# Expert bias parts: formed on VectorE from biases loaded ahead of the expert pieces, instead of by ScalarE and GpSimd in turns

## The chip, the cores and the metric

One core of a Trainium2 chip runs the whole kernel. Its engines each follow their own list of instructions and meet at semaphores: TensorE (PE in the profile) multiplies, VectorE (DVE) and ScalarE (ACT) work element by element, GpSimd (POOL) builds small tables and starts some transfers, and SyncE (SP) does nothing but wait and start transfers. The metric is the device time of one execution in microseconds (us), taken as the median of several executions.

## The reference

One layer of a transformer is run for two groups of tokens that share their weights: 256 prompt tokens and 64 sample tokens with 512 cached keys. Everything is float32.

```python
x = x + mixed @ w_o                       # mixed: two kinds of attention heads, concatenated
h = rmsnorm(x, g_ffn)                     # 320 tokens of width 1024
logits = h @ w_r + b_r                    # 32 experts, the best 4 of each token are used
for e in range(32):
    g = min(h @ w_gate[e] + b_gate[e], 7)
    u = clip(h @ w_up[e] + b_up[e], -7, 7)
    y = ((u + 1) * (g * sigmoid(1.702 * g))) @ w_down[e] + b_down[e]
    x += combine[:, e] * y
x = x + (p @ w_ple_proj) * sigmoid(rmsnorm(x, g_ple) @ w_ple_gate)
return rmsnorm(x, g_final), and the new keys, values and log-forget rows
```

Each of the three expert matrices has 4 MB per expert, so 32 experts hold some 400 MB that have to be read once from HBM.

## The kernel before

The program has three stages: projections and attention (0 to about 216 us of the profile), output projection and routing (216 to 304 us), and the experts (304 to 1299 us) with a short tail.

**Experts.** An item is up to 64 tokens of one expert. Its weights come as six pieces of 2 MB (two of the gate matrix, two of up, two of down) into a ring of six slots; `early` holds two more. SP starts the load of a piece as soon as PE has used the piece that lay in the slot (`wait_used`, semaphore `piece_used`). Of the first item, pieces 0, 1, 2 and 5 can be loaded once attention has left their slots; pieces 3 and 4 lie where `w_o` is kept, so that they, and behind them in SP's list the two early pieces of the second item, wait for the whole output projection (`wo_ps` 6).

**Biases.** The rows of `b_gate`, `b_up` and `b_down` are added by a matmul. Its stationary operand `sel` picks the expert, its moving operand `bparts` holds all biases as three bfloat16 parts that add up to the float32 value: partitions 0 to 31, 32 to 63 and 64 to 95 each hold one part of the 32 experts' 3072 biases. So SP loads three copies of the biases into `bias32` (nine transfers of 128 KB, lines 409 to 411). A first copy rounds all 96 rows to bfloat16 (`bias_part` 1). Then the rounded values are subtracted in place on the first 64 rows and these are rounded again, and the same once more on the first 32 rows. Before the change ScalarE rounds (lines 685 to 690) and GpSimd subtracts (lines 528 to 531); each waits for the other (`bias_part`, `bias_rest`). `bias32` and `bparts` lie in `area`, where attention keeps its queries and keys, so they can only be filled when PE has read those for the last time.

**What stands around them.** Every engine works through its list in the order in which it is written. On GpSimd the two subtractions stand ahead of the small tables of the routing (lines 533 to 546), the last of which raises `consts` to 3. On VectorE the last work of attention is `new_key_rows` (lines 1191 to 1197), which copies the transposed new keys out; then comes a wait for `consts` 3 (line 1314), three small copies into `ident_e`, and `add_out` (line 1287), which adds a block of the output projection to `X`. On PE the order is: three blocks of the output projection (`project_out`), the transposes of `normed_to_T(0)` (line 952), which need both `add_out` of the first 128 tokens, the fourth block, `logits`, and so on to the routing, the first `gather` of tokens and the first item. On ScalarE `squares` for the norm follow behind the bias copies.

**SP** in this stretch: the two loads of `w_o`, a wait for all ten transfers of new keys and values to the outputs (`out_dma`), piece 0, a wait for the end of attention, pieces 1, 2, 5, the nine biases, a wait for `wo_ps` 6, pieces 3, 4 and the two early ones.

Of the kernel before, what the change touches and what calls it, by code (L numbers as in the profile page):

```python
# [31 lines left out]
ALU = mybir.AluOpType  # L32
ACT = mybir.ActivationFunctionType
# [3 lines left out]
D = 1024  # L37
# [15 lines left out]
NE, TOPK = 32, 4  # L53
# [40 lines left out]
def build(nc, A, O):  # L94
    ctx = ExitStack()
    with ctx:
# [3 lines left out]
        def sem(name):  # L100
            return ctx.enter_context(nc.semaphore(name))
# [37 lines left out]
        def cut(n):  # L139
            nonlocal a  # L140
            a += n
            return area[:, a - n:a]
# [4 lines left out]
        bias32 = area[0:3 * NE, 0:3 * D]  # L147
        bparts = cut(3 * D // 2)[0:3 * NE, :].bitcast(BF16).rearrange("p (r n) -> p r n", r=3)
# [81 lines left out]


        x_in, g_in, small_in, kc_in, vc_in, ff_in, tab_in = [sem(n) for n in ("x_in", "g_in", "small_in", "kc_in", "vc_in", "ff_in", "tab_in")]
        bias_in, bias_part, bias_rest, rel_out, rel_rows, rel_in, out_dma = [sem(n) for n in ("bias_in", "bias_part", "bias_rest", "rel_out", "rel_rows", "rel_in", "out_dma")]
        wqk = [sem(f"wqk{i}") for i in range(CHUNK_SLOTS)]
        wv_in, wout_in = sem("wv_in"), sem("wout_in")
        consts = sem("consts")
# [9 lines left out]
        kr_ps, kr_sb = sem("kr_ps"), sem("kr_sb")  # L246
# [95 lines left out]
        def down(tile, n):  # L342

            return tile[n * SLOTS:(n + 1) * SLOTS, :]

        @block.sync
        def _(sp):
# [23 lines left out]
            def load(e, s, into=None, done=None):  # L371

                src = wexp[s // 2][bass.ds(e, 1), s % 2].rearrange("a p c n -> (a p) c n") if not isinstance(e, int) else wexp[s // 2][e, s % 2]
                sp.dma_start((ring if into is None else into)[:, s, :].rearrange("p (c n) -> p c n", c=QC), src).then_inc((done or wst)[s], 16)  # L374
# [25 lines left out]
                sp.dma_start(wout[h], w_o[:, :, h * GW:(h + 1) * GW]).then_inc(wout_in, 16)  # L400


            sp.wait_ge(out_dma, OUT_PRE)
            load(0, 0)
            sp.wait_ge(mixed_ok, 1)
            sp.wait_ge(o_ps, NO)
            for s in (1, 2, 5):
                load(0, s)
            for r, nm in enumerate(("b_gate", "b_up", "b_down")):
                for k in range(3):  # L410
                    sp.dma_start(bias32[k * NE:(k + 1) * NE, r * D:(r + 1) * D], A[nm][0]).then_inc(bias_in, 16)  # L411
            sp.wait_ge(wo_ps, 2 * NT)
            for s in (3, 4):
                load(0, s)
# [42 lines left out]
        def _(pool):  # L457
            g = nc.gpsimd
            n = 0
# [56 lines left out]
            for t in range(NT):  # L516
                r = ROWS[t]
# [6 lines left out]
            for x, nm in ((0, "fk"), (1, "dk")):  # L524
                g.dma_start(O[nm + "_p"][0, 0].rearrange("(t p) h -> p t h", p=P), krow[x][:, 0:2, :]).then_inc(out_dma, 16)
                g.dma_start(O[nm + "_s"][0, 0], krow[x][0:DEC, 2, :]).then_inc(out_dma, 16)

            for k in (2, 1):
                pool.wait_ge(bias_part, 3 - k)
                v = bias32[0:k * NE, :]  # L530
                g.tensor_tensor(v, v, bparts[0:k * NE, :, :].rearrange("p r n -> p (r n)"), ALU.subtract).then_inc(bias_rest, 1)  # L531

            pool.wait_ge(o_sb, NO)
            g.iota(iota_s, [[1, SLOTS]], base=1, channel_multiplier=0, allow_small_or_imprecise_dtypes=True)
# [9 lines left out]
            for h in range(2):  # L544
                ins = g.memset(down(far[:, :], h), float(2 * FAR + h))
# [17 lines left out]
            for t in range(NT):  # L563
                r = ROWS[t]
# [8 lines left out]
        def _(act_e):  # L573
            s = nc.scalar
            n = 0
# [106 lines left out]
            for j, c in enumerate((4, 5, 6, 7, 0, 1, 2, 3)):  # L682
                act_e.wait_ge(hT_ps, DC + j + 1)
                s.activation(hT[:, c, :], ps[:, c, 0:NTOK], ACT.Copy).then_inc(hT_sb, 1)
            parts = bparts.rearrange("p r n -> p (r n)")
            act_e.wait_ge(bias_in, 16 * 9)
            s.activation(parts, bias32, ACT.Copy).then_inc(bias_part, 1)
            for k in (2, 1):
                act_e.wait_ge(bias_rest, 3 - k)
                s.activation(parts[0:k * NE, :], bias32[0:k * NE, :], ACT.Copy).then_inc(bias_part, 1)  # L690
            for t in range(NT):
                act_e.wait_ge(x1_ok, 2 * (t + 1))
                squares(1, t)
# [1 line left out]
            for t in range(NT):  # L695
                r = ROWS[t]
# [29 lines left out]
            for t in range(NT):  # L726
                r = ROWS[t]
# [17 lines left out]
            for t in range(NT):  # L745
                r = ROWS[t]
# [11 lines left out]
        def _(pe):  # L758
# [31 lines left out]
            for t in range(NT):  # L790
                r = ROWS[t]
# [227 lines left out]
            def tokens(i):  # L1019

                pe.wait_ge(rows_sb, lin(i, 1, 1))
                columns_of(tok_rows, TOK_BANK).then_inc(tokT_ps, 1)
# [18 lines left out]
            def trip(i):  # L1041

                pe.wait_ge(tok_ok, lin(i, 1, 1))
                pe.wait_ge(sel_ok, lin(i, 1, 1))
                bias(0, G_BANK)
                product(i, 0, tokT, G_BANK)
                if i is FIRST:
                    tables()
                product(i, 1, tokT, G_BANK)
                bias(1, U_BANK)  # L1050
                product(i, 2, tokT, U_BANK)
                product(i, 3, tokT, U_BANK)
                if i is not FIRST:
                    pe.wait_ge(y_sb, lin(i, 1))
                bias(2, Y_BANK)
                gather(item(i, 1))
                pe.wait_ge(act_ok, lin(i, 1, 1))
                columns_of(act, ACT_BANK).then_inc(actT_ps, 1)
                tokens(item(i, 1))
                pe.wait_ge(actT_ok, lin(i, 1, 1))  # L1060
                product(i, 4, actT, Y_BANK)
                product(i, 5, actT, Y_BANK)
# [11 lines left out]
            mm(ps[:, TAB_BANK, 100:101], below[:, :], need, True, True)  # L1074
            mm(ps[0:1, TAB_BANK, 101:102], need, ones[:, 0:1], True, True).then_inc(rank_ps, 1)
            tokens(FIRST)
            pe.wait_ge(bias_part, 3)
            trip(FIRST)
            pe.wait_ge(items_ok, 1)
            n1 = pe.value_load(cnti[0:1, 0:1], min_val=NE - 1, max_val=ITEMS - 1)  # L1080
# [5 lines left out]
            for c in range(2):  # L1086
                for t in range(NT):
                    r = ROWS[t]
# [27 lines left out]
            for t in range(NT):  # L1116
                r = ROWS[t]
# [19 lines left out]
        def _(dve):  # L1137
            V = nc.vector
            n = 0

            def link(ins):

                nonlocal n
                n += 1
                ins.then_inc(dve_seq, 1)
                dve.wait_ge(dve_seq, n)
# [20 lines left out]
            for t in range(NT):  # L1167
                r = ROWS[t]
                ins = V.tensor_tensor(zz[0:r, t, :], ps[0:r, 6, t * FH:(t + 1) * FH], bf[0:r, :], ALU.add)
# [5 lines left out]
            for i in range(2):  # L1175
                ins = V.tensor_tensor(dlam[:, 128 * i:128 * i + 64], dlam[:, 128 * i:128 * i + 64], dlam[:, 128 * i + 64:128 * i + 128], ALU.mult)
# [14 lines left out]
            def new_key_rows():  # L1191
                for g8 in range(8):
                    x, m = g8 // 4, g8 % 4
                    dve.wait_ge(kr_ps, g8 + 1)
                    V.tensor_copy(krow[x][:, 0:2, m * P:(m + 1) * P],
                                  ps[:, g8 % 4, 0:2 * P].rearrange("p (t n) -> p t n", t=2)).then_inc(kr_sb, 1)
                    V.tensor_copy(krow[x][0:DEC, 2, m * P:(m + 1) * P], ps[0:DEC, g8 % 4, 2 * P:3 * P]).then_inc(kr_sb, 1)
# [58 lines left out]
            for p in range(PAIRS):  # L1256
# [4 lines left out]
                if p == 5:  # L1261

                    dve.wait_ge(o_sb, DH)
                    for t in range(NT):
                        r = ROWS[t]
                        if t == 2:
                            dve.wait_ge(sub_ss, 1)
                        for hh in range(DH):
                            v = H[0:r, t, GW + hh * P:GW + (hh + 1) * P]
                            ins = V.scalar_tensor_tensor(squares_of[0:r, t % 2, hh * P:(hh + 1) * P], v, 1.0, v, ALU.mult, ALU.mult,  # L1270
                                                         accum_out=ssd[0:r, t, hh:hh + 1])
                        ins.then_inc(sub_ss, 1)
                if p == 6:
                    dve.wait_ge(sub_rstd, NT)
                    for t in range(NT):
                        r = ROWS[t]
                        for hh in range(DH):
                            v = H[0:r, t, GW + hh * P:GW + (hh + 1) * P]
                            ins = V.scalar_tensor_tensor(v, v, ssd[0:r, t, hh:hh + 1], subg[0:r, :], ALU.mult, ALU.mult)
                    ins.then_inc(mixed_ok, 1)  # L1280
            new_key_rows()

            def add_out(t, h):
                r = ROWS[t]
                dve.wait_ge(wo_ps, 2 * t + h + 1)
                src = ps[0:r, 2 * t + h, :] if t < 2 else down(ps[:, 4, :], h)
                V.tensor_tensor(X[0:r, t, h * GW:(h + 1) * GW], src, X[0:r, t, h * GW:(h + 1) * GW], ALU.add).then_inc(x1_ok, 1)
# [27 lines left out]
            for k in range(3):  # L1315
                rr = slice(k * NE, (k + 1) * NE)
                ins = V.tensor_copy(ident_e[rr, :], ident[rr, rr])
# [16 lines left out]
            for t in range(NT):  # L1334
                r = ROWS[t]
                ins = V.tensor_reduce(place[0:r, t, :], masks[0:r, :, t, :].rearrange("p k e -> p e k"), AXX, ALU.add)
            link(ins)
            for t in range(NT):
                r = ROWS[t]
                ins = V.tensor_scalar(slotv[0:r, t, 0:NE], place[0:r, t, :], -1.0, tok4[0:r, t:t + 1], ALU.mult, ALU.add)  # L1340
# [4 lines left out]
            for t in range(NT):  # L1345
                r = ROWS[t]
                ins = V.scalar_tensor_tensor(posm[0:r, t, 0:NE], ps[0:r, POS_BANKS[t], t * NE:(t + 1) * NE], 1.0, mask[0:r, t, :], ALU.add, ALU.mult)
# [64 lines left out]
            for t in range(NT):  # L1412
                r = ROWS[t]
                dve.wait_ge(w_exp, t + 1)
                link(V.reciprocal(wsum[0:r, 2, t:t + 1], wsum[0:r, 1, t:t + 1]))
                ins = V.tensor_scalar(w4[0:r, t, :], w4[0:r, t, :], wsum[0:r, 2, t:t + 1], None, ALU.mult)
# [35 lines left out]
            for t in range(NT):  # L1452
                r = ROWS[t]
                dve.wait_ge(pj_sb, t + 1)
                for h in range(2):
# [3 lines left out]
                    ins = V.tensor_tensor(X[0:r, t, c], tsig[0:r, c], X[0:r, t, c], ALU.add)  # L1459
# [44 lines left out]
```

## Time and profile before

| | us |
|---|---|
| median of three executions | 1383.2 (1380.15 to 1385.09) |
| profiled execution | 1379.01 |
| its span, first to last instruction | 1377.2 |
| PE busy in the span | 1207.5 (88%) |
| DVE, ACT, POOL busy | 296.5, 189.0, 87.9 |
| read from HBM | 469.32 MB, 351 GB/s over the span |

The profile page gives shares over the whole span; the stages differ. In its row of 40 slices (34.4 us each) the transfers run at 427 to 430 GB/s from the 13th slice to the 36th, and at 5 GB/s in the eighth. A wait in brackets in the timeline is idle time of that engine before the instruction, with what ended it.

### The profile page before, as it was taken

The numbers are of one execution on the slowest core, as the hardware profiler recorded it, in microseconds if no ns is written. First come the engines' busy times: TensorE is split into PE (matmuls) and PEld (weight loads), VectorE is DVE, ScalarE is ACT, GpSimd is POOL, SyncE is SP. The second block draws the span as 40 slices with busy tenths as digits, with TensorE's granted clock in tenths as the row PEclk, the third lists the DMA queues.
The fourth block names the chain that finished last, engine by engine and source line by source line (L and its number), as shares of the span: only waits on it lengthen the run. The fifth ranks groups of instructions, "written<-read, shape, count | busy, mean of one in ns | idle before, by whom it ended". The sixth has DMA issues, their size and how long they took to land.

```text
span 1377.2 us, 15632 instructions
## 1 busy us (share of the span) xinstructions
PE 1207.5 (88%) x5919; PEld 496.2 (36%) x5919; DVE 296.5 (22%) x844; ACT 189.0 (14%) x419; POOL 87.9 (6%) x148
## 2 busy tenths in 40 slices
PE   5999979489999899988898988889998889998866
PEld 4565664243333333332233332233333223333322
DVE  2343450142211111111111111111111111111153
ACT  2232441210100010000001000001000000100122
POOL 6000100400000000000000000000000000000000
PEclk9999987789999999999999999999999999999978
DMA  9460158059999999999999999999999999999941
GB/s 294 172 168 16 51 186 312 5 245 371 396 429 427 428 430 429 428 429 429 428 429 429 429 428 428 428 428 429 429 428 427 430 429 429 428 427 428 369 150 39
DMA packets 64555, 478.88 MB, mean 348 GB/s; under 512 B 9136, under 2 KB 26136, under 8 KB 38100
## 3 DMA queue, kind: packets, MB, share of 16 engines
q1 hardware_dynamic: 57968, 462.19, 81.1%
q0 software_dynamic: 4496, 16.02, 3.2%
q10 hardware_dynamic: 2068, 0.37, 0.2%
q8 instruction: 14, 0.23, 0.1%
q14 instruction: 9, 0.07, 0.0%
HBM read 469.32 MB, written 14.47 MB: 351 GB/s over the span
## 4 chain that ended last, share of the span: by engine, by line
DMA 58%; PE 35%; DVE 2%; POOL 1%; ACT 1%; issue 1%; SPq 1%; ACTq 0%; POOLq 0%; DVEq 0%
DMA ring<-in_w_up 54%; PE ps L762 33%; DMA area<-in_b_down 2%; POOL area L531 1%; DMA ring<-expert_rows 1%; PE ps L774 1%; DMA X<-in_x_sample 0%; DMA expert_rows<-area,rowi 0%; DVE X L1437 0%; DMA out_dk_s<-ring 0%; PE ps L1016 0%; PE ps L871 0%; PE ps L873 0%; SPq L374 0%; SPq L411 0%
## 5 line engine op out<-in xcount | busy, mean ns | idle before, releaser
L762 PE MATMUL ps<-ring,area 128*64 128x512 f32 x3232 | 728.0, 597 | 93.3 <-DMA ring<-in_w_up 76.8
L762 PEld LDWEIGHTS ps<-ring,area 128*64 128x64 f32 x3232 | 221.8, 137 | 556.2 <-issue 383.8
L1381 DVE TENSOR_SCALAR area<-ps 128x512 f32<-128x512 f32 x34 | 23.5, 691 | 429.4 <-PE ps L762 429.4
L762 PE MATMUL ps<-ring,hT 128*128 128x512 f32 (+2 forms) x320 | 110.9, 570 | 2.8 <-issue 2.3
L762 PE MATMUL ps<-H,area 128*64 128x512 f32 (+1 forms) x420 | 103.1, 609 | 2.5 <-DVE area L1355 2.5
L558 POOL DMA_INDIRECT expert_rows<-area,rowi x34 | 33.2, 977 | 979.7 <-ACT area L715 979.7
L762 PE MATMUL ps<-area 128*64 128x1 f32 (+6 forms) x756 | 79.0, 285 | 1.7 <-issue 1.2
L1385 DVE TENSOR_SCALAR area<-ps 128x512 f32<-128x512 f32 x34 | 23.5, 692 | 259.5 <-PE ps L762 259.5
L762 PE MATMUL ps<-hT,ring 128*128 128x320 f32 x256 | 74.9, 448 | 0.0
L704 ACT ACTIVATE area<-ps 128x512 f32<-128x512 f32 x35 | 20.9, 597 | 393.4 <-PE ps L762 393.4
L762 PEld LDWEIGHTS ps<-ring,hT 128*128 128x128 f32 (+1 forms) x320 | 46.9, 176 | 61.7 <-issue 58.8
L762 PEld LDWEIGHTS ps<-area 128*64 128x64 f32 (+4 forms) x756 | 38.3, 134 | 66.3 <-issue 64.4
L709 ACT ACTIVATE area<-area 128x512 f32<-128x512 f32 x34 | 21.4, 629 | 264.8 <-DVE area L1381 264.8
L762 PEld LDWEIGHTS ps<-hT,ring 128*128 128x128 f32 x256 | 48.8, 195 | 24.1 <-issue 6.2
L715 ACT ACTIVATE area<-ps 128x512 f32<-128x512 f32 x34 | 20.3, 597 | 244.4 <-PE ps L762 244.4
L762 PEld LDWEIGHTS ps<-H,area 128*64 128x64 f32 (+1 forms) x420 | 27.2, 137 | 65.7 <-issue 63.1
L1016 PE MATMUL ps<-ident,area 128*128 128x128 f32 x276 | 42.5, 297 | 0.0
L1016 PEld LDWEIGHTS ps<-ident,area 128*128 128x128 f32 x276 | 35.9, 210 | 0.5
L1383 DVE TENSOR_TENSOR area<-area 128x512 f32<-128x512 f32 x34 | 23.6, 693 | 23.6 <-ACT area L709 23.6
L1355 DVE TENSOR_SCALAR area<-area 128x64 f32<-128x64 f32 (+1 forms) x108 | 27.0, 308 | 0.9
L660 ACT ACTIVATE ring<-ring,mx 128x128 f32<-128x128 f32 (+2 forms) x48 | 26.3, 552 | 6.7 <-DVE mx L1231 6.6
L762 PE MATMUL ps<-ring 128*128 128x64 f32 (+3 forms) x96 | 17.1, 309 | 10.2 <-ACT ring L643 10.2
(193 smaller groups left out, 556.0 us busy)
## 6 DMA issues: line engine op xcount, KB each, us to landing
ring<-in_w_up SPq DMA_DIRECT2D x68, 2048.0 KB, 25.8
ring<-in_w_down SPq DMA_DIRECT2D x68, 2048.0 KB, 22.6
ring<-in_w_gate SPq DMA_DIRECT2D x66, 2048.0 KB, 25.2
ring<-in_w_in SPq DMA_DIRECT2D x16, 512.0 KB, 8.4
ring<-in_w_in SPq DMA_DIRECT2D x2, 2048.0 KB, 9.6
ring<-in_w_o SPq DMA_DIRECT2D x2, 2048.0 KB, 15.1
early<-in_w_gate SPq DMA_DIRECT2D x2, 2048.0 KB, 19.0
ring<-in_w_ple_gate SPq DMA_DIRECT2D x1, 4096.0 KB, 31.6
```

Source lines behind the costliest of these rows:

```text
L531: g.tensor_tensor(v, v, bparts[0:k * NE, :, :].rearrange("p r n -> p (r n)"), ALU.subtract).then_inc(bias_rest, 1)
L558: g.indirect_dma_start(out=yscr[:, :], out_offset=bass.IndirectOffsetOnAxis(ap=rowi[:, 0:1], axis=0), in_=yrow, in_offset=None, bounds_che ...
L660: last = s.activation(v, v, ACT.Exp, bias=mx[0:r, u, t:t + 1], accum_out=rs[0:r, u, t:t + 1])
L704: s.activation(tok_rows, ps[:, ROWS_BANK, :], ACT.Copy).then_inc(rows_sb, 1)
L709: s.activation(sig, gate, ACT.Sigmoid, scale=ALPHA).then_inc(sig_ok, 1)
L715: s.activation(yrow, ps[:, Y_BANK, :], ACT.Copy).then_inc(y_sb, 1)
L762: return T.matmul(out, lhsT, rhs, start=first, stop=last)
L1016: last = T.transpose(ps[:, b, c * P:(c + 1) * P], rows[:, c::QC], ident[:, :])
L1355: ins = V.tensor_scalar(pick[0:r, t, :], iota_s[0:r, :], posm[0:r, t, bass.ds(e, 1)], first[0:r, bass.ds(lin(i, 1), 1)], ALU.subtract, ALU ...
L1381: V.tensor_scalar(gate, ps[:, G_BANK, :], LIMIT, None, ALU.min).then_inc(g_sb, 1)
L1383: V.tensor_tensor(gate, gate, sig, ALU.mult)
L1385: V.tensor_scalar(up, ps[:, U_BANK, :], LIMIT, -LIMIT, ALU.min, ALU.max).then_inc(up_sb, 1)
```

## The change

SP starts the nine bias loads behind the loads of `w_o`, as soon as PE has made the last transposes of the new keys (`kr_ps` 8), and in front of the wait for `out_dma` and all expert pieces. VectorE makes the three roundings and the two subtractions, in a row behind `new_key_rows` and in front of the wait for `consts` 3. ScalarE and GpSimd have none of it, the semaphore `bias_rest` goes, and PE waits for one signal of `bias_part` in place of three. Data, sizes and all other work stay.

```diff
+            sp.wait_ge(kr_ps, 8)
+            for r, nm in enumerate(("b_gate", "b_up", "b_down")):
+                for k in range(3):
+                    sp.dma_start(bias32[k * NE:(k + 1) * NE, r * D:(r + 1) * D], A[nm][0]).then_inc(bias_in, 16)
             sp.wait_ge(out_dma, OUT_PRE)
             load(0, 0)
             sp.wait_ge(mixed_ok, 1)
             sp.wait_ge(o_ps, NO)
             for s in (1, 2, 5):
                 load(0, s)
-            for r, nm in enumerate(("b_gate", "b_up", "b_down")):
-                for k in range(3):
-                    sp.dma_start(bias32[k * NE:(k + 1) * NE, r * D:(r + 1) * D], A[nm][0]).then_inc(bias_in, 16)
             sp.wait_ge(wo_ps, 2 * NT)
...
-            for k in (2, 1):
-                pool.wait_ge(bias_part, 3 - k)
-                v = bias32[0:k * NE, :]
-                g.tensor_tensor(v, v, bparts[0:k * NE, :, :].rearrange("p r n -> p (r n)"), ALU.subtract).then_inc(bias_rest, 1)
-
             pool.wait_ge(o_sb, NO)
...
-            parts = bparts.rearrange("p r n -> p (r n)")
-            act_e.wait_ge(bias_in, 16 * 9)
-            s.activation(parts, bias32, ACT.Copy).then_inc(bias_part, 1)
-            for k in (2, 1):
-                act_e.wait_ge(bias_rest, 3 - k)
-                s.activation(parts[0:k * NE, :], bias32[0:k * NE, :], ACT.Copy).then_inc(bias_part, 1)
             for t in range(NT):
                 act_e.wait_ge(x1_ok, 2 * (t + 1))
                 squares(1, t)
...
-            pe.wait_ge(bias_part, 3)
+            pe.wait_ge(bias_part, 1)
             trip(FIRST)
...
             new_key_rows()
 
+            parts = bparts.rearrange("p r n -> p (r n)")
+            dve.wait_ge(bias_in, 16 * 9)
+            link(V.tensor_copy(parts, bias32))
+            for k in (2, 1):
+                v = bias32[0:k * NE, :]
+                link(V.tensor_tensor(v, v, parts[0:k * NE, :], ALU.subtract))
+                ins = V.tensor_copy(parts[0:k * NE, :], v)
+                if k == 2:
+                    link(ins)
+            ins.then_inc(bias_part, 1)
```

SyncE's list from the loads of `w_o` to the biases, before; `in_w_gate`, `in_w_up` and `in_w_down` into `ring` are expert pieces, `in_b_...` the biases:

```order
L400 DMA ring<-in_w_o 128x8x512 x2
L374 DMA ring<-in_w_gate 128x4096 x2
L374 DMA ring<-in_w_up 128x4096
L374 DMA ring<-in_w_down 128x4096
L411 DMA area<-in_b_gate 32x1024 x3
L411 DMA area<-in_b_up 32x1024 x3
L411 DMA area<-in_b_down 32x1024 x3
```

The same place of SyncE's list after the change:

```order
L400 DMA ring<-in_w_o 128x8x512 x2
L406 DMA area<-in_b_gate 32x1024 x3
L406 DMA area<-in_b_up 32x1024 x3
L406 DMA area<-in_b_down 32x1024 x3
L374 DMA ring<-in_w_gate 128x4096 x2
L374 DMA ring<-in_w_up 128x4096
L374 DMA ring<-in_w_down 128x4096
```

The nine biases have moved past four pieces, which are 8 MB; nothing else has moved.

VectorE's list from the last copies of `new_key_rows` to `add_out`, before:

```order
L1195 COPY ring<-ps 128x2x128
L1197 COPY ring<-ps 64x128
L1317 COPY area<-ident 32x32 x3
L1319 MEMSET area 128x54
L1287 TENSOR_TENSOR X<-ps,X 128x512 x3
```

The same place after the change:

```order
L1185 COPY ring<-ps 128x2x128
L1187 COPY ring<-ps 64x128
L1275 CAST area<-area 96x3072
L1278 TENSOR_TENSOR area<-area 64x3072
L1279 CAST area<-area 64x3072
L1278 TENSOR_TENSOR area<-area 32x3072
L1279 CAST area<-area 32x3072
L1318 COPY area<-ident 32x32 x3
L1320 MEMSET area 128x54
L1288 TENSOR_TENSOR X<-ps,X 128x512 x3
```

Five instructions over 3072 columns have come in front of the copies into `ident_e`; what follows is as it was.

## Rows read from the trace of the kernel before

**Rows 1.** The page: the chain that ended last, by engine.
```profile
DMA 58%; PE 35%; DVE 2%; POOL 1%; ACT 1%; issue 1%; SPq 1%; ACTq 0%; POOLq 0%; DVEq 0%
```

**Rows 2.** The chain in order of time: start us, us, what.
```profile
425.12 23.58 DMA ring<-in_w_up
...
1257.39 25.96 DMA ring<-in_w_up
```

**Rows 3.** Windows: stretch and length, busy us by engine, granted PE clock, DMA, GB/s.
```profile
247.10:265.30 18.20, 0.00 (x0) 0.00 (x0) 1.31 (x6) 5.53 (x2) 12.96 (x21) 0.65 0.00 0
265.30:269.60 4.30, 4.25 (x11) 2.78 (x12) 2.42 (x3) 1.15 (x2) 0.76 (x2) 0.50 0.00 0
269.60:285.10 15.50, 15.50 (x72) 7.38 (x70) 5.39 (x16) 1.15 (x2) 0.75 (x2) 1.00 0.00 1
285.10:306.00 20.90, 15.65 (x96) 9.89 (x98) 11.59 (x50) 4.09 (x10) 0.73 (x2) 0.70 0.96 397
306.00:310.00 4.00, 4.00 (x20) 1.53 (x18) 0.13 (x1) 0.00 (x0) 0.00 (x0) 0.86 0.07 25
...
350.00:360.00 10.00, 9.80 (x54) 4.06 (x54) 1.99 (x8) 1.39 (x3) 0.00 (x0) 1.00 0.90 347
```

**Rows 4.** Timeline of PE: start us, us, instruction [idle before, releaser].
```profile
202.97 3.85 PE L902 MATMUL ps<-ident,area 128*128 128x128 f32 x24
...
223.87 23.21 PE L762 MATMUL ps<-ring,hT 128*128 128x512 f32 x48 [0.53 <-ACT hT L684]
265.35 1.97 PE L952 MATMUL ps<-ident,X 128*128 128x128 f32 x8 [18.28 <-DVE X L1287]
...
296.39 4.81 PE L762 MATMUL ps<-H,area 128*64 128x512 f32 x12 [2.48 <-DVE area L1355]
...
304.41 4.96 PE L762 MATMUL ps<-ring,area 128*64 128x512 f32 x16
...
320.56 2.89 PE L762 MATMUL ps<-H,area 128*64 128x512 f32 x12
```

**Rows 5.** Timeline of DVE.
```profile
263.87 0.54 DVE L1317 COPY area<-ident 32x32 f32<-32x32 f32 x3 [55.53 <-POOL far L545]
...
264.61 1.89 DVE L1287 TENSOR_TENSOR X<-ps,X 128x512 f32<-128x512 f32 x3
```

**Rows 6.** Timeline of ACT.
```profile
242.73 2.76 ACT L687 ACTIVATE area<-area 96x3072 bf16<-96x3072 f32 x1 [18.91 <-DMA area<-in_b_down]
```

**Rows 7.** Timeline of POOL.
```profile
210.63 0.55 POOL L526 DMA_DIRECT2D out_dk_s<-ring  x1
245.58 5.99 POOL L531 TENSOR_TENSOR area<-area 64x3072 f32<-64x3072 f32 x1 [34.40 <-ACT area L687]
...
260.38 0.18 POOL L534 IOTA area<- 128x64 f32 x1
...
263.61 0.23 POOL L545 MEMSET far<- 64x1 f32 x2
```

**Rows 8.** Timeline of SP's queue.
```profile
217.61 1.47 SPq L411 DMA_DIRECT2D area<-in_b_gate  x3
...
285.07 0.35 SPq L374 DMA_DIRECT2D ring<-in_w_up  x1
...
309.40 4.38 SPq L374 DMA_DIRECT2D ring<-in_w_gate  x2
```

**Rows 9.** Lines of DVE, 180 to 310 us: busy us, mean ns, idle before.
```profile
L1293 DVE TENSOR_TENSOR hT<-ps,gT 128x1024 f32<-128x1024 f32 x2 | 2.5, 1225 | 2.1 <-PE ps L952 2.1
...
L1152 DVE TENSOR_SCALAR H<-X,ss 128x1024 f32<-128x1024 f32 x2 | 1.5, 746 | 0.0
```

**Rows 10.** DMA issues, 200 to 250 us: KB each, median us to landing.
```profile
area<-in_b_down SPq DMA_DIRECT2D x3, 128.0 KB, 21.2
...
out_dk_s<-ring POOLq DMA_DIRECT2D x1, 128.0 KB, 5.0
```

**Rows 11.** Windows as in rows 3: the end of the bias loads.
```profile
238.00:240.00 2.00, 2.00 (x6) 0.85 (x5) 0.00 (x0) 0.00 (x0) 0.00 (x0) 1.00 1.01 246
```

More of the change, by code:

```diff
@@ L232, in build @@
         x_in, g_in, small_in, kc_in, vc_in, ff_in, tab_in = [sem(n) for n in ("x_in", "g_in", "small_in", "kc_in", "vc_in", "ff_in", "tab_in")]
-        bias_in, bias_part, bias_rest, rel_out, rel_rows, rel_in, out_dma = [sem(n) for n in ("bias_in", "bias_part", "bias_rest", "rel_out", "rel_rows", "rel_in", "out_dma")]
+        bias_in, bias_part, rel_out, rel_rows, rel_in, out_dma = [sem(n) for n in ("bias_in", "bias_part", "rel_out", "rel_rows", "rel_in", "out_dma")]
         wqk = [sem(f"wqk{i}") for i in range(CHUNK_SLOTS)]
```

## The prediction

> **What bounds the kernel now.** I read the chain by engine first: 58% of the span is transfers, 35% TensorE [rows 1]. In order of time this splits into stages. From 425 us to the end of the last item the chain is nothing but the wait for the next piece of weights, 29 times some 26 us, and the matmuls behind it [rows 2]; no engine's speed matters there. What counts before is when that stream of pieces starts and when it was last held up. So I read the windows: from 247.1 to 285.1 us the transfers stand still (0 to 1 GB/s), from 285.1 they run at 397 GB/s for 20.9 us, rest for most of 306 to 310 us, rest once more around 353 us (0.90 of the stretch), and never again [rows 3]. Each of these starts is an act of TensorE: at 285.07 us the last block of the output projection lets SyncE load pieces 3 and 4 and the two early ones, and at 309.40 us the first used piece lets it go on [rows 8]. The rest at 353 us has the same cause, slots that TensorE has not yet freed. So an edit that lets TensorE reach these two points earlier moves the whole stream, and the stream carries the shift to the end.
>
> TensorE's own timeline shows one large hole there: after the three blocks of the projection, which end at 223.87 + 23.21 = 247.08 us, it stands for 18.28 us until VectorE's `add_out` has run [rows 4]. VectorE did not compute in this time. It waited 55.53 us for the last of GpSimd's small tables, and reached `add_out` at 264.61 us [rows 5]. GpSimd was late because of the biases: they landed at about 242.7 us, ScalarE rounded (2.76 us), GpSimd subtracted (5.99 us), and so on in turns, until GpSimd began its tables at 260.38 us and ended them at 263.84 us [rows 6, 7]. The tables themselves wait only for the end of attention, about 216 us.
>
> **What the change removes.** GpSimd's two subtractions and ScalarE's three roundings leave the path to `consts` 3. With GpSimd free at the end of attention (about 216 us) the tables, 260.38 to 263.84 us = 3.5 us [rows 7], are done at about 219.5 us.
>
> **What it adds and moves.** First the loads. SyncE now waits for the last transposes of the keys. These end on TensorE at 202.97 + 3.85 = 206.8 us [rows 4], so the nine issues start at about 207 us, and with the pace of before (three in 1.47 us [rows 8]) the last is out at 211.4 us. Nothing is lost by this wait: what is queued behind it on SyncE, piece 0, waits for the outputs of the keys, whose last was issued at 210.6 us and landed 5.0 us later, at 215.6 [rows 7, 10]. The biases now share the transfer engines with these outputs. Nine times 128 KB are 1.18 MB; they moved at 246 GB/s when they were alone at the end [rows 11], that is 4.8 us. Landing then lies between 211.4 + 5.0 = 216.4 us (a small transfer on its own) and 211.4 + 21.2 = 232.6 us (as before, behind 8 MB) [rows 10]. I take the outputs first, to 215.6 us, and then the biases: 220.4 us. If it is the other way round, the outputs land at 220.4 us and the expert pieces behind them start up to 4.8 us later; their 8 MB, at 397 GB/s [rows 3] 21 us, are there by about 242 us, and the first item uses them past 280 us. So this costs nothing.
>
> Then the five instructions on VectorE, all over 3072 columns. No row shows one of them there. The nearest for a rounding is the tensor-scalar over 1024 columns, 746 ns, three times that is 2.24 us; the nearest for a subtraction is the two-operand form over 1024 columns, 1225 ns, so 3.68 us [rows 9]. That gives 3 x 2.24 + 2 x 3.68 = 14.1 us. Lower end: all five at 2.24, 11.2 us. Upper end: all at GpSimd's 5.99 us, 30.0 us. I take 14.1, since those rows are of the engine itself. VectorE is idle from 263.87 - 55.53 = 208.3 us on [rows 5], so it forms the parts from 220.4 to 234.5 us, copies `ident_e` (0.74 us from 263.87 to 264.61) and stands at `add_out` at 235.2 us. Behind its new wait are queued just these and everything of the routing; who waits for them are TensorE at line 952 and ScalarE's `squares`.
>
> TensorE needs the two `add_out` of the first 128 tokens by 247.08 us. Two take 1.26 us (1.89 us for three [rows 5]), so VectorE may come as late as 245.8 us. It has 10.6 us to spare; this cover hides the whole of the added work. PE's wait for `bias_part` stands in front of the first item, past 280 us, and is long fulfilled.
>
> **The sum.** The hole goes: 18.28 us [rows 4]. What is late next at 247.08 us is nothing: TensorE goes on without a stop. The clock adds a little. Its granted level was 1.00 up to 247.1 us, fell in the hole (mean 0.65), and was 0.50, the lower of its two levels, from 265.3 to 269.6 us while TensorE worked [rows 3]. Without the hole those 4.3 us of work should run at 1.00: half, 2.15 us. All later steps to 285 us (the fourth block, the logits, the sample rows, the routing) keep their order and waits. So both starts of the stream come 18.28 + 2.15 = 20.4 us earlier, and so does the end.
>
> Against the profiled execution: 1379.01 - 20.4 = 1358.6 us, 1356.8 of it span (1.8 us lie around it). That execution is 4.2 us below the median, which gives 1383.2 - 20.4 = 1362.8 us for a median. I forecast 1362, near the latter.
>
> **Size of the uncertain terms.** The clock falls again in the routing: the first gather took 4.81 us where a later one takes 2.89, and the first product of the first item 4.96 us for what is worth about 3.5 at the full level [rows 4]; this fall may come earlier or later by a few us when the work ahead is not interrupted. If it does not come at all, 1.9 + 1.5 = 3.4 us more are gained; if it comes before the last logits, up to 2.5 us are lost. So the gain is 18 to 24 us, the time 1358 to 1365 us by the median, and with the spread of the three executions 1357 to 1367.
>
> **Rivals.** *VectorE becomes the gate, and the time is slower than before.* If the biases land as late as before after their issue, 232.6 us, and the five instructions take 30.0 us, VectorE ends at 262.6 us. If GpSimd then cannot write its tables while VectorE works, their 3.5 us and the 0.74 us of `ident_e` come on top: `add_out` at 266.8 us against 264.61, 2.2 us later than before, 1385.4 us. It decides from the point where VectorE reaches `add_out`: no loss up to 245.8 us, 1 us for each us beyond, slower than before from 264.6 us. For it speaks that VectorE's list now holds a wait for a transfer in the middle of the path; against it that no 8 MB stand in front of the biases now, and that rows of VectorE itself are at a third to two thirds of GpSimd's time. The Trainium skill (GPSIMD Engine Reference, section Specifications) says that GpSimd shares its SBUF interfaces with VectorE, with contention when a VectorE instruction has two SBUF inputs or runs in a two-port mode. All five are of such kinds, and the tables fall into their time. No row here shows this; it would hold the tables back to 238.0 us at most, still before 245.8, so by this rule the sum stays and only this rival grows, by the 3.5 us named.
>
> *VectorE is late in part.* Landing at 232.6 us with 14.1 us of work gives `add_out` at 247.4 us, 1.6 us lost (1364 us); with 30.0 us of work from 220.4 us it is 251.1 us, 5.3 us lost (1368 us). A loss of 6 to 15 us (1369 to 1378) needs something of both.
>
> *The front is hidden.* If the stream set its own end, with its start given by something that does not move, the time stays at 1383. For it speaks the share of 58% for transfers, against it the idle transfers between 247.1 and 285.1 us, which end with an act of TensorE [rows 3, 8].
>
> *TensorE's hole is only moved.* If the routing behind 247 us met a wait that the hole had hidden, for instance ScalarE's `squares` and GpSimd's power for the norm, it would cost some us. Both are free from 224 us on and their inputs come with `add_out`, so I see at most 2 us, 1364.
>
> **How the numbers follow.** Forecast with its own range (1357 to 1367): 0.85, the moved wait in it. VectorE late in part, more than 4 us lost: 0.08. Front hidden: 0.03. VectorE so late that it is slower: 0.02. The remaining 0.02 is for a slower stream of which no row tells. What a measurement of this kernel can tell from no change is about 0.3%, 4.1 us. Faster: 0.85 + 0.08 + a little = 0.94; same 0.03; slower 0.03. The range is 1356 to 1368: it takes in the clock's part and a few us of VectorE's lateness.
>
> **What would show it.** In the profile after: the biases land before 225 us; five VectorE instructions between about 217 and 236 us, in all 11 to 18 us; no wait of GpSimd between attention and its tables; line 952 on TensorE starts at about 247 us with under 1 us of idle time; the granted clock is 1.00 from 230 to 265 us; four pieces are issued at about 265 us and the first freed slot at about 289 us; the waits for weights from then on are the same, 20 us earlier. Wrong would be a hole in front of line 952 ended by VectorE, or a start of the stream that comes 20 us earlier with an end that does not.

## The result, and the profile after

| | before | changed |
|---|---|---|
| median of four executions, us | 1384.14 (1380.15 to 1385.23) | 1360.90 (1358.41 to 1363.40) |
| span of the profiled execution, us | 1377.2 | 1357.0 |

The changed kernel takes 0.9837 of the time of before, 95% interval 0.9806 to 0.9869. In two later groups of runs, each with its own runs of the kernel before, the ratio was 0.9860 (0.9839 to 0.9881) and 0.9844 (0.9826 to 0.9862). The forecast was 1362 us, in a range of 1356 to 1368. Between the two profiled executions the span shrank by 20.2 us, where 20.4 were forecast.

The lines that answer to the rows of before, in the order of the steps. SyncE's queue after (start us, us, what), beside [rows 8]:

```profile
207.02 1.26 SPq L406 DMA_DIRECT2D area<-in_b_gate  x3
208.32 1.35 SPq L406 DMA_DIRECT2D area<-in_b_up  x3
209.71 2.79 SPq L406 DMA_DIRECT2D area<-in_b_down  x3
218.52 0.83 SPq L374 DMA_DIRECT2D ring<-in_w_gate  x2
...
264.67 0.33 SPq L374 DMA_DIRECT2D ring<-in_w_up  x1
...
289.06 4.39 SPq L374 DMA_DIRECT2D ring<-in_w_gate  x2
```

The biases go out from 207 us on. The first pieces start at 218.5 us, 2.9 us later than before, which costs nothing, since the transfers rest from 247 us on (below). The two starts of the stream of weights, 285.07 and 309.40 us before, are at 264.67 and 289.06: 20.4 and 20.3 us earlier.

VectorE's timeline after, beside [rows 5]; behind the tile names stand partitions x elements and type:

```profile
216.71 1.80 DVE L1275 CAST area<-area 96x3072 bf16<-96x3072 f32 x1 [8.21 <-DMA area<-in_b_down]
218.54 3.35 DVE L1278 TENSOR_TENSOR area<-area 64x3072 f32<-64x3072 f32 x1
221.93 1.75 DVE L1279 CAST area<-area 64x3072 bf16<-64x3072 f32 x1
223.71 3.35 DVE L1278 TENSOR_TENSOR area<-area 32x3072 f32<-32x3072 f32 x1
227.09 1.75 DVE L1279 CAST area<-area 32x3072 bf16<-32x3072 f32 x1
228.77 0.53 DVE L1318 COPY area<-ident 32x32 f32<-32x32 f32 x3
229.38 0.10 DVE L1320 MEMSET area<- 128x54 f32 x1
233.54 0.69 DVE L1288 TENSOR_TENSOR X<-ps,X 128x512 f32<-128x512 f32 x1 [4.06 <-PE ps L752]
```

The biases land at 216.7 us. The five instructions take 12.1 us from start to end, and then it is VectorE that waits, for TensorE (4.06 us). The copies into `ident_e` no longer wait for GpSimd.

TensorE's timeline after, beside [rows 4]:

```profile
224.03 23.21 PE L752 MATMUL ps<-ring,hT 128*128 128x512 f32 x48 [0.53 <-ACT hT L680]
247.07 1.04 PE L942 MATMUL ps<-ident,X 128*128 128x128 f32 x8
247.95 7.03 PE L752 MATMUL ps<-ring,hT 128*128 128x512 f32 x16
```

Line 942 is line 952 of before. It has no bracket: the hole of 18.28 us is gone. The transposes take 1.04 us where they took 1.97. The windows say why (columns as in [rows 3]):

```profile
247.24:264.67 17.43, 17.43 (x81) 8.63 (x80) 7.27 (x18) 1.15 (x2) 0.75 (x2) 1.00 0.00 1
264.67:285.00 20.33, 15.09 (x96) 9.77 (x98) 11.62 (x50) 4.09 (x10) 0.73 (x2) 0.71 0.96 395
```

TensorE is busy for all of the first stretch, at a granted clock of 1.00. In the routing the clock falls as before (mean 0.71). Behind it the chain is the old one, shifted: its last wait for a piece, 25.96 us long at 1257.39 us before, is

```profile
1237.21 25.96 DMA ring<-in_w_up
```

### The profile page after: what moved, and what is told of

It reads as the page before. It is cut to its first block, busy times and chain, and to the rows that moved or that the text cites. A ratio compares the mean times of both kernels' runs of the same rounds, so it can differ in the third digit from the quotient of the medians.

```text
span 1357.0 us, 15632 instructions
## 1 busy us (share of the span) xinstructions
PE 1205.2 (89%) x5919; PEld 494.9 (36%) x5919; DVE 308.6 (23%) x849; ACT 180.7 (13%) x416; POOL 77.5 (6%) x146
## 4 chain that ended last, share of the span: by engine, by line
DMA 57%; PE 38%; DVE 2%; ACT 1%; issue 1%; POOL 0%; SPq 0%; ACTq 0%; POOLq 0%; DVEq 0%
DMA ring<-in_w_up 55%; PE ps L752 35%; PE ps L764 1%; DMA ring<-expert_rows 1%; DMA X<-in_x_sample 0%; DMA expert_rows<-area,rowi 0%; DVE X L1438 0%; PE ps L861 0%; PE ps L863 0%; PE ps L1006 0%; PE ps L892 0%; PE ps L1088 0%; ACT H L587 0%; DVE area L1152 0%; ACT area L702 0%
## 5 line engine op out<-in xcount | busy, mean ns | idle before, releaser
L705 ACT ACTIVATE area<-ps 128x512 f32<-128x512 f32 x34 | 20.3, 597 | 244.4 <-PE ps L752 244.4
## 6 DMA issues: line engine op xcount, KB each, us to landing
early<-in_w_gate SPq DMA_DIRECT2D x2, 2048.0 KB, 18.9
```

Of the source, the lines that this page charges most:

```text
L705: s.activation(yrow, ps[:, Y_BANK, :], ACT.Copy).then_inc(y_sb, 1)
```

## The experiments

The theory: the gain is the hole in front of line 942, made by GpSimd's late tables; whoever keeps VectorE from being late at `add_out` gets it, and the stream of weights carries it to the end. The rivals: the engine that forms the parts decides; the place of the loads decides; all added work on VectorE counts.

The table has two measures. The time is the median. The stage is the time in the profile from the start of the output projection (the matmuls x48 at 223.87 us before) to the issue of the first freed slot (309.40 us before). It leaves out what happens ahead of it, which differs between executions by some us. Each ratio is to runs of the kernel before made in the same group.

| kernel | median us | ratio to before, 95% interval | stage us |
|---|---|---|---|
| before | 1384.14 | 1 | 85.53 |
| changed | 1360.90 | 0.9837 [0.9806, 0.9869] | 65.03 |
| changed, second time | 1360.98 | 0.9860 [0.9839, 0.9881] | 65.04 |
| changed, third time | 1360.07 | 0.9844 [0.9826, 0.9862] | 64.88 |
| e1 early load only | 1363.05 | 0.9855 [0.9838, 0.9873] | 64.46 |
| e2 VectorE only | 1371.61 | 0.9918 [0.9900, 0.9936] | 75.51 |
| e3 tables first | 1369.58 | 0.9894 [0.9871, 0.9917] | 71.79 |
| e4 pieces ahead | 1362.22 | 0.9856 [0.9835, 0.9878] | 65.53 |
| e5 six more roundings | 1360.98 | 0.9856 [0.9834, 0.9877] | 65.04 |
| e6 twelve more roundings | 1369.34 | 0.9904 [0.9885, 0.9922] | 71.96 |
| e7 busy routing | 1360.41 | 0.9852 [0.9831, 0.9872] | 64.79 |
| e8 busy, trimmed | 1357.68 | 0.9829 [0.9809, 0.9849] | 61.90 |
| e9 busy, attention too | 1353.08 | 0.9798 [0.9780, 0.9816] | 61.29 |

**e1, early load only.** The loads of the change, on the kernel before:

```diff
+            sp.wait_ge(kr_ps, 8)
+            for r, nm in enumerate(("b_gate", "b_up", "b_down")):
+                for k in range(3):
+                    sp.dma_start(bias32[k * NE:(k + 1) * NE, r * D:(r + 1) * D], A[nm][0]).then_inc(bias_in, 16)
             sp.wait_ge(out_dma, OUT_PRE)
...
-            for r, nm in enumerate(("b_gate", "b_up", "b_down")):
-                for k in range(3):
-                    sp.dma_start(bias32[k * NE:(k + 1) * NE, r * D:(r + 1) * D], A[nm][0]).then_inc(bias_in, 16)
             sp.wait_ge(wo_ps, 2 * NT)
```

> The kernel before with one edit: the nine bias loads stand in front of the expert pieces; ScalarE and GpSimd form the parts in turns as before. Main theory (the gain is the hole in front of line 952 that GpSimd's late tables make, whoever forms the parts): biases land at about 217 us, ScalarE starts behind its hT copies at 224 us, the five steps take 17.7 us and end, with the last subtraction, at about 242 us, the tables at 245.4, add_out starts at about 246.2 us and line 952 at about 247.3: a hole under 1 us, and a time within 1 us of the changed kernel, 1361 to 1362 us. Rival (forming on VectorE is what gives): the hole stays near 18 us and the time near 1384 us.

The hole is gone and the stage is as short as that of the changed kernel (64.46 against 65.03 us). VectorE's timeline shows how narrowly:

```profile
247.38 0.54 DVE L1318 COPY area<-ident 32x32 f32<-32x32 f32 x3 [36.37 <-POOL far L546]
248.11 1.89 DVE L1288 TENSOR_TENSOR X<-ps,X 128x512 f32<-128x512 f32 x3
```

and TensorE's next instruction behind the projection has no wait:

```profile
249.10 1.04 PE L953 MATMUL ps<-ident,X 128*128 128x128 f32 x8
```

VectorE still waits for GpSimd, but only to 247.38 us. TensorE's projection, which started 2.4 us later here than in the changed kernel, ends at 249.3 us, when the first `add_out` is there and the second about to be. The later start did not help: ScalarE's first rounding follows its last copy into `hT` without a wait (226.23 us), the projection waits for the same copy (226.39 us), so that both shift together. So the engine is not what gave the time. Forming on VectorE turned a cover that just reaches into one with some 16 us to spare (229.5 against 245.8 us). The median lies 1 us above the expected 1361 to 1362; the intervals of the ratio overlap.

**e2, VectorE only.** The changed kernel with the nine loads back behind pieces 1, 2 and 5:

```diff
-            sp.wait_ge(kr_ps, 8)
-            for r, nm in enumerate(("b_gate", "b_up", "b_down")):
-                for k in range(3):
-                    sp.dma_start(bias32[k * NE:(k + 1) * NE, r * D:(r + 1) * D], A[nm][0]).then_inc(bias_in, 16)
             sp.wait_ge(out_dma, OUT_PRE)
...
+            for r, nm in enumerate(("b_gate", "b_up", "b_down")):
+                for k in range(3):
+                    sp.dma_start(bias32[k * NE:(k + 1) * NE, r * D:(r + 1) * D], A[nm][0]).then_inc(bias_in, 16)
             sp.wait_ge(wo_ps, 2 * NT)
```

> The changed kernel with the nine bias loads back behind pieces 1, 2 and 5; VectorE forms the parts. Main theory: biases land at 242.7 us, the five steps take 12.1 us (as in the changed kernel's profile), ident_e 0.7, add_out at 255.6 us, line 952 at about 256.4 us with 9 us of idle time in front; with up to 2.1 us at the lower clock behind it the time is 9 to 11.5 us above the changed kernel: 1370 to 1372.5 us. Rival (the place of the loads is worth nothing, the engine everything): 1361 us. Rival (the early load is everything): 1384 us.

```profile
255.83 1.97 PE L941 MATMUL ps<-ident,X 128*128 128x128 f32 x8 [8.71 <-DVE X L1287]
```

A hole of 8.71 us, a stage 10.5 us longer, 1371.6 us: as expected. Of the 18.28 us of the hole, forming on VectorE alone takes away about half, the early load alone all.

**e3, tables first.** The kernel before, with GpSimd's two subtractions moved:

```diff
-            for k in (2, 1):
-                pool.wait_ge(bias_part, 3 - k)
-                v = bias32[0:k * NE, :]
-                g.tensor_tensor(v, v, bparts[0:k * NE, :, :].rearrange("p r n -> p (r n)"), ALU.subtract).then_inc(bias_rest, 1)
             pool.wait_ge(o_sb, NO)
...
             ins.then_inc(consts, 1)
+            for k in (2, 1):
+                pool.wait_ge(bias_part, 3 - k)
+                v = bias32[0:k * NE, :]
+                g.tensor_tensor(v, v, bparts[0:k * NE, :, :].rearrange("p r n -> p (r n)"), ALU.subtract).then_inc(bias_rest, 1)
             pool.wait_ge(consts, 3)
```

> The kernel before with one edit: GpSimd makes its routing tables before the two subtractions and not behind them; loads and steps of the biases as before. Main theory (a full queue ahead of the tables, not the bias work as such): line 952 starts at about 247.2 us without a hole, but ScalarE's squares for the norm still stand behind its third rounding (263.2 us), so that VectorE's scaled rows of the first tokens wait to about 266 us where the changed kernel has 255.6, and the routing and the first item come 5 to 8 us later than in the changed kernel: 1366 to 1369 us. Rival (the biases have to be ready before the routing goes on): 1383 to 1384 us.

VectorE in this kernel:

```profile
224.57 0.54 DVE L1317 COPY area<-ident 32x32 f32<-32x32 f32 x3 [11.12 <-POOL far L540]
...
260.00 0.69 DVE L1287 TENSOR_TENSOR X<-ps,X 128x512 f32<-128x512 f32 x1 [5.64 <-PE ps L762]
270.44 0.76 DVE L1152 TENSOR_SCALAR H<-X,ss 128x1024 f32<-128x1024 f32 x1 [9.76 <-POOL ss L488]
```

and TensorE, whose projection started at 228.96 us:

```profile
252.05 1.04 PE L952 MATMUL ps<-ident,X 128*128 128x128 f32 x8
```

The tables are early and line 952 has no hole, though the biases land as late as before (18.9 us behind the start of the projection in both kernels) and ScalarE and GpSimd do the same work. A new wait of 9.76 us stands behind it: ScalarE's `squares` is queued behind its third rounding. The stage is 6.8 us longer than that of the changed kernel, inside the expected 5 to 8. So the late parts as such hold nothing up here; the instructions queued behind them do. The median is 0.6 us above its range. The profiled execution (1370.61 us) started the projection at 229.0 us against 224.0, which the stage leaves out; whether the other three started late too is not recorded.

**e5 and e6, more work on VectorE.** The first rounding made 7 and 13 times:

```diff
-            link(V.tensor_copy(parts, bias32))
+            for _ in range(7):        # e6: 13
+                link(V.tensor_copy(parts, bias32))
```

> The changed kernel with the first rounding made 7 times, 6 x 1.83 = 11 us more work on VectorE. Main theory: parts done at 239.8 us, add_out at 240.5 us, still ahead of 245.8 us: no hole, same time as the changed kernel within 0.5 us. Rival (added work on VectorE shows): up to 1372 us.

> The changed kernel with the first rounding made 13 times in place of once, 12 x 1.83 = 22 us more work on VectorE. Main theory (the cover ends where add_out must start at 245.8 us): the parts are done at 250.7 us, add_out starts at 251.5 us, line 952 at 252.2 us with a hole of about 5 us; with the clock 1366 to 1369 us. GpSimd's small memsets, if a rounding of VectorE keeps them from their memory as the first one did for 1.5 us, come late, up to 240 us, and that too must not matter more than this. Rival (all of VectorE's work is hidden): 1361 us. Rival (every added us counts): 1383 us.

VectorE in e5, then TensorE in e6:

```profile
240.97 1.29 DVE L1289 TENSOR_TENSOR X<-ps,X 128x512 f32<-128x512 f32 x2
246.95 0.69 DVE L1289 TENSOR_TENSOR X<-ps,X 128x512 f32<-128x512 f32 x1 [4.69 <-PE ps L752]
```

```profile
254.50 1.92 PE L942 MATMUL ps<-ident,X 128*128 128x128 f32 x8 [5.32 <-DVE X L1289]
```

11 us more cost nothing; 22 us more make a hole of 5.32 us and a stage 6.9 us longer. So the cover ends between the two, as the prediction had it, and behind its end each us counts: in e6, in e2 and in the kernel before, the hole is what is left from the end of the projection (249.18, 247.1 and 247.08 us) to 0.74 us behind the start of `add_out` (253.76, 255.08 and 264.61 us). The 1.6 us beyond the hole fit the clock, which is 0.69 in the 5.5 us behind the hole.

**e4, pieces ahead.** The changed kernel with the two early pieces in front of the wait for the projection:

```diff
+            for s in range(2):
+                load(1, s, early, ahead)
             sp.wait_ge(wo_ps, 2 * NT)
             for s in (3, 4):
                 load(0, s)
-            for s in range(2):
-                load(1, s, early, ahead)
```

> The changed kernel with the two early pieces of the second item issued in front of the wait for the output projection, so that 4 MB move while the transfers stand still (242 to 265 us) and only pieces 3 and 4 are left for 265 us. Theory A (of the stream's two starts the one at the first freed slot, 289 us, carries the shift; all slots are full by then either way): same time within 0.5 us. Theory B (the start at 265 us carries it): 4 MB at 428 GB/s, 9.8 us less: 1351 us.

No gain, as theory A had it, where theory B asked for 9.8 us less: the stage is 0.5 us longer than that of the changed kernel run beside it, and the median 1.2 us above it, with intervals that overlap. How much is moved at the first start does not count: in both kernels the transfers rest before the first slot is freed (0.01 of the engines' time from 285 us to the issue at 292.49 us in e4).

**e7, e8 and e9, the clock.** The prediction gave 3.4 us to the fall of the granted clock in the routing. e7 fills TensorE's waits there with matmuls whose results nobody reads:

```diff
+            def warm(n):
+                for _ in range(n):
+                    mm(ps[:, 0, 128:512], ident[:, :], X[:, 0, 0:384], True, True)
+
+            pe.wait_ge(x1_ok, 2 * NT)
+            warm(3)
             logits(2)
...
+                if (t, t2) == (1, 1):
+                    warm(2)
                 positions(t, t2)
...
+            warm(2)
             positions(2, 2).then_inc(pos_ps, 1)
             counts(2).then_inc(need_ps, 1)
+            warm(6)              # e8: warm(1)
```

> The changed kernel with 13 matmuls without use (128 x 384, results not read) in TensorE's waits of the routing, 3 before the last logits, 2 and 2 between the position matmuls, 6 before the first gather. Theory (the fall of the granted clock at about 269.6 us costs the first gather 1.9 us and the first product 1.5 us, and comes from little work on TensorE in the routing): the clock stays at 1.00 and the time falls by 1 to 3 us, since the 13 matmuls also cost up to 1 us. Rival (the fall has another cause): the clock falls as before, and the time is the same or up to 3 us longer.

The clock stayed at 1.00 and the time did not move. The window of the routing and TensorE's timeline in e7:

```profile
266.00:285.00 19.00, 17.84 (x104) 10.68 (x106) 10.45 (x48) 3.65 (x10) 0.72 (x2) 1.00 0.99 420
```

```profile
274.64 4.14 PE L752 MATMUL ps<-X,ident 128*128 128x384 f32 x12
278.71 2.94 PE L752 MATMUL ps<-H,area 128*64 128x512 f32 x12
```

The gather takes 2.94 us, as at the full level, but starts late: the six matmuls (two instructions each) run to 278.7 us, while VectorE's last result that the gather needs is there at 275.7. I had taken all 13 for at most 1 us; they run 0.69 us each.

> As e7_busy_routing, with 1 matmul without use before the first gather in place of 6 (8 in all). In e7 the six ran to 278.7 us while their end was waited for from 275.7 us on. Theory (the clock's fall in the routing costs 3.4 us, and e7 gave it back in those 3 us): the granted clock stays at 1.00 and the stretch from line 942 to the first gather shrinks by 3 us: 3 us under the changed kernel. Rival (the fall comes back with fewer matmuls): the first gather at 4.8 us again, same time as the changed kernel.

```profile
278.62 2.94 PE L752 MATMUL ps<-H,area 128*64 128x512 f32 x12 [0.27 <-DVE area L1367]
...
284.60 3.63 PE L752 MATMUL ps<-ring,area 128*64 128x512 f32 x16
```

These are TensorE's gather and the first product of the first item; in the changed kernel run beside it the two take 4.80 and 4.96 us. The stage is 3.0 us shorter. The median is 2.4 us lower, which the intervals alone don't separate.

e9 adds the same at the end of attention, in the bank that the next values go to:

```diff
-                pe.wait_ge(pt_sb, i + 1)
                 b = out_bank(i)
...
+                if i >= 8:
+                    for _ in range(7 if i == 8 else 1):
+                        mm(ps[:, b, 0:384], ident[:, :], X[:, 0, 0:384], True, True)
+                pe.wait_ge(pt_sb, i + 1)
```

> As e8_busy_trimmed, and in addition 10 such matmuls at the end of attention (7 in TensorE's wait at 189 to 194.7 us, 1 in each of three later waits of 0.95 us), written into the bank that the next values go to. Theory (the lower level of the clock from 190.5 to 204.7 and 211.8 to 228.6 us comes from that wait): the clock stays at 1.00, TensorE's work there runs at the full level; the transposes at 216 us (7.38 us) lose 3 us, the projection's first part 2.3 us, the rest up to 4 us: 5 to 9 us under e8. Rival (the stretch is bound by ScalarE and VectorE): at most 3 us under e8.

Windows of e8, then of e9:

```profile
206.00:216.00 10.00, 8.10 (x61) 6.89 (x59) 4.40 (x16) 2.70 (x11) 2.54 (x4) 0.84 0.58 173
216.00:230.00 14.00, 12.67 (x40) 6.56 (x41) 9.88 (x4) 4.21 (x11) 4.01 (x19) 0.50 0.77 298
```

```profile
206.00:216.00 10.00, 8.98 (x65) 5.99 (x63) 1.65 (x7) 4.17 (x15) 4.05 (x15) 1.00 0.77 251
216.00:230.00 14.00, 13.47 (x40) 6.35 (x39) 13.20 (x10) 2.48 (x6) 2.54 (x8) 1.00 0.97 393
...
266.00:285.00 19.00, 17.57 (x87) 7.35 (x87) 6.90 (x35) 1.88 (x2) 0.00 (x0) 0.91 0.87 354
```

The clock stays up through the end of attention and the projection: the transposes in front of the projection take 4.65 us in place of 7.38, the projection's first part 20.87 in place of 23.17. It does not stay up to the end of the stage. The clock, 1.00 in e8 through the first product of the first item, is 0.68 here from 275.1 to 280.5 us, and the product takes 5.32 us in place of 3.63:

```profile
275.15 5.32 PE L752 MATMUL ps<-ring,area 128*64 128x512 f32 x16
```

So of the 2.3 us that the stage gains in the projection it gives 1.7 back; why the clock falls there and not in e8, no run shows. The median falls by 4.6 us, a little less than the expected 5 to 9. With a ratio of 0.9798 against 0.9844 of the changed kernel on the same chip, intervals apart, e9 beats both kernels.

## Why the prediction was right

**The bound.** Right. The second start of the stream and its end moved by the same 20.3 and 20.2 us. The text gave the shift to both starts; e3 and e8 show that the second alone carries it. SyncE's queue in e3, then in e8:

```profile
269.65 0.35 SPq L374 DMA_DIRECT2D ring<-in_w_up  x1
...
300.75 4.38 SPq L374 DMA_DIRECT2D ring<-in_w_gate  x2
```

```profile
266.96 0.33 SPq L374 DMA_DIRECT2D ring<-in_w_up  x1
...
288.25 4.39 SPq L374 DMA_DIRECT2D ring<-in_w_gate  x2
```

Counted from the start of the projection, the first start lies at 40.6 to 40.7 us in both, as in the changed kernel, and the second at 71.79 and 61.90 us against 65.03. The end of the span follows the second: it lies between 1067.6 and 1068.2 us behind it in all thirteen profiles, while behind the first it lies 1099.2 us in e3 and 1088.9 us in e8.

**The hole.** 18.28 us were to go, and all went. The cause named, GpSimd's tables behind the subtractions, is shown by e3: the tables alone, moved ahead, remove the hole. What e3 also shows, and the sum did not need, is a second queue behind the biases, ScalarE's `squares`; it would have taken 6.8 us back had only the tables been moved. The rival that the hole is only moved was at work there, and the change avoids it by emptying both queues.

**The clock.** 2.15 us were forecast for the stretch behind the hole; with the hole that made 20.4 us. Measured are 0.93 us in the transposes (1.97 to 1.04) and 1.23 in the fourth block (8.26 to 7.03), which before was

```profile
267.12 8.26 PE L762 MATMUL ps<-ring,hT 128*128 128x512 f32 x16
```

and the first start of the stream came 285.07 - 264.67 = 20.4 us earlier. The term of the routing (3.4 us) did not change with this change: the fall came as before. e8 shows that its size was right, 3.0 us in the stage.

**The added work.** The landing, taken at 220.4 us, came at 216.7: outputs and biases shared the engines and took less together than one after the other. The five instructions took 12.1 us where 14.1 were taken. Both errors lay under the cover. Its end, 245.8 us, was set some 0.5 us too early. The prediction asked for both `add_out` of the first 128 tokens before line 952, as does the text ahead of it, but the transposes wait for them one at a time (the first four need only the first): in the rows of before, line 952 starts 0.74 us behind the start of `add_out`, not 1.26. With 16 us to spare this changed nothing.

**The rivals.** VectorE did not become the gate. With 11 us more work it still is not (e5); with 22 us more it is, and costs 5 to 7 us (e6). The rule of the Trainium skill (GPSIMD Engine Reference, section Specifications) was weighed there with 3.5 us, at most 238 us for the tables. GpSimd after:

```profile
216.71 0.18 POOL L534 IOTA area<- 1x54 f32 x1
216.95 1.59 POOL L537 MEMSET area<- 32x1 f32 x1
218.60 0.20 POOL L538 MEMSET area<- 32x128 f32 x1
...
220.87 0.23 POOL L541 MEMSET far<- 64x1 f32 x2
```

One memset that takes 0.09 us elsewhere took 1.59 us and ended with VectorE's first rounding (218.5 us); the rest ran at their usual pace beside VectorE's subtraction. That section of the Trainium skill names two inputs as well, so by it the subtraction should have held them up too; beside these memsets and iotas, which read no tile, it did not, and the measurement decides. The tables ended at 221.1 us.

**The time.** In the stage the shift was 20.50, 20.49 and 20.65 us in the changed kernel's three profiles, where 20.4 were forecast. That the spans of the first two profiles agree with the sum to 0.2 us is in part luck, since the changed kernel's other two profiles have spans of 1358.7 and 1358.6 us, 18.5 us under that of before. So it is with the median's 23.2 us in the first comparison: the later two give 19.2 and 21.7 us.

## What to carry to other kernels

A chain that two engines pass back and forth cost more here by what was queued behind its links than by its own length: list what stands behind each waiting instruction on every engine that takes part, since moving only one of these queues uncovers the next (e3). A small load that gates such work belongs in front of the bulk loads, and here that alone gave the whole gain (e1). When a hole is removed, reckon the work behind it at the full clock, and set the point up to which added work is hidden, so that an experiment can test it.

## What the runs showed of the hardware

A rounding on VectorE (float32 to bfloat16, one input) held up GpSimd's memsets and iotas on the same memory. In e6, with 13 roundings in a row, GpSimd's timeline reads

```profile
219.65 1.74 POOL L538 MEMSET area<- 32x128 f32 x1
221.46 1.61 POOL L539 IOTA area<- 32x1 f32 x1
223.13 0.09 POOL L537 MEMSET area<- 32x1 f32 x1
223.28 1.70 POOL L538 MEMSET area<- 32x128 f32 x1
```

so three instructions get through in two roundings of 1.8 us each: two of the three are held up, and one of 0.09 us slips in between. The subtraction, with two inputs, did not hold up the same instructions (0.09 to 0.23 us each beside it). They read no tile; how a GpSimd instruction that reads one or two fares beside it is not shown here.

On VectorE a rounding of 3072 columns took 1.75 us and a subtraction 3.35 us, whatever the number of partitions (96, 64 and 32 for the rounding, 64 and 32 for the subtraction). Before, ScalarE took 2.76 us for the rounding and GpSimd 5.99 us for the subtraction.

Unexpected was also how much of the spread between executions lies ahead of the change: the projection started between 223.5 and 229.0 us in the twelve profiles other than that of e9, while the stage behind it was the same to 0.2 us in the changed kernel's three (64.88 to 65.04). In e9, with TensorE kept busy at the end of attention, it started at 219.2 us. What else sets that start was not tried.
